# Head norms of mixers AB and C: the reciprocal root as exp of minus half the logarithm, on ScalarE

## What is computed

```python
def _head_rmsnorm(o, gain):
    o = o * lax.rsqrt(jnp.mean(o * o, axis=-1, keepdims=True) + NORM_EPS)
    return o.reshape(o.shape[0], o.shape[1], -1) * gain.astype(jnp.float32)

# mixer AB: ob = _head_rmsnorm(ob, norm_gain); y = concat([oa, ob]) * silu(gate); y @ w_out
# mixer C:  y = _head_rmsnorm(o, norm_gain) * silu(gate);                        y @ w_out
```

## Time and profile before

| | us |
|---|---|
| runs of the kernel | 2100.96, 2101.53, 2105.75; median 2101.53 |
| the profiled execution | 2103.88, of which the span from first to last instruction 2101.8 |
| mixer AB from the first scan's decays to the layer norm | about 1700 to 1804 of the span |
| mixer C | about 1804 to the end |
| mean granted PE clock over the span | 0.961 |

### The profile page before, as it was taken

One profiled execution on the slowest core, in us unless ns is written; L12 is line 12 of the kernel. 1 busy time (PEld: TensorE's weight loads), 2 busy tenths in 40 slices (PEclk: granted clock), 3 DMA queues, 4 the chain that ended last, 5 costly groups with the idle time before them and its releaser, 6 DMA issues.

```text
span 2101.8 us, 31282 instructions
## 1 busy us (share of the span) xinstructions
PE 1939.4 (92%) x12015; PEld 1628.8 (77%) x12015; DVE 1177.1 (56%) x1900; ACT 962.4 (46%) x1437; POOL 147.3 (7%) x172
## 2 busy tenths in 40 slices
PE   5999998999997999999898999899989998789996
PEld 3875665688886888888765789799878787789994
DVE  3335566343345555523545556677644578669895
ACT  3336444322224434411446555466435454566761
POOL 3010000000000222210000000022200000000000
PEclk7999999999997999999999999899999999899998
DMA  9225568233331332333340057445564333334432
GB/s 299 93 83 165 176 205 251 70 90 103 94 116 45 100 100 95 99 108 98 100 121 1 11 143 187 155 160 180 189 216 141 101 121 120 121 121 141 141 121 80
DMA packets 262663, 265.88 MB, mean 127 GB/s; under 512 B 6278, under 2 KB 230896, under 8 KB 262560
## 3 DMA queue, kind: packets, MB, share of 16 engines
q1 hardware_dynamic: 257280, 248.27, 37.9%
q0 software_dynamic: 4832, 15.06, 2.2%
q10 hardware_dynamic: 448, 1.12, 0.2%
HBM read 263.33 MB, written 1.10 MB: 126 GB/s over the span
## 4 chain that ended last, share of the span: by engine, by line
PE 74%; DVE 11%; ACT 8%; issue 3%; DMA 2%; SPq 0%; ACTq 0%; DVEq 0%; POOL 0%
PE bank L474 19%; PE bank L475 19%; PE bank L476 19%; PE bank L694 4%; PE bank L710 3%; DVE weights_fine L1743 3%; ACT weights_coarse L1100 2%; PE bank L468 2%; PE bank L521 2%; PE bank L532 2%; DMA region<-in_w_mod 2%; PE bank L701 1%; PE bank L738 1%; DVE region L2332 1%; ACT L1496 1%
## 5 line engine op out<-in xcount | busy, mean ns | idle before, releaser
L1743 DVE TENSOR_TENSOR weights_fine<-region,weights_coarse 128x2048 fp32r<-128x2048 f32 (+3 forms) x187 | 431.8, 2309 | 392.4 <-ACT weights_coarse L1100 391.7
L1100 ACT CAST weights_coarse<-region 128x2048 fp32r<-128x2048 f32 (+3 forms) x187 | 358.7, 1918 | 361.0 <-PE bank L476 340.3
L474 PE MATMUL bank<-normed_coarse,weights_coarse 128*128 128x512 f32 (+1 forms) x1088 | 368.5, 339 | 14.3 <-DVE normed_fine L1851 9.1
L475 PE MATMUL bank<-normed_fine,weights_coarse 128*128 128x512 f32 (+1 forms) x1088 | 367.4, 338 | 0.0
L476 PE MATMUL bank<-normed_coarse,weights_fine 128*128 128x512 f32 (+1 forms) x1088 | 367.3, 338 | 0.0
L474 PEld LDWEIGHTS bank<-normed_coarse,weights_coarse 128*128 128x128 f32 x1088 | 208.0, 191 | 38.2 <-issue 13.5
L475 PEld LDWEIGHTS bank<-normed_fine,weights_coarse 128*128 128x128 f32 x1088 | 208.0, 191 | 21.5
L476 PEld LDWEIGHTS bank<-normed_coarse,weights_fine 128*128 128x128 f32 x1088 | 207.9, 191 | 21.4
L474 PE MATMUL bank<-x_turned_coarse,weights_coarse 128*128 128x256 f32 x616 | 181.9, 295 | 22.5 <-DVE weights_fine L1743 17.6
L475 PE MATMUL bank<-x_turned_fine,weights_coarse 128*128 128x256 f32 x616 | 178.9, 290 | 0.0
L476 PE MATMUL bank<-x_turned_coarse,weights_fine 128*128 128x256 f32 x616 | 178.7, 290 | 0.0
(11 more groups left out here) (278 smaller groups left out, 3718.2 us busy)
## 6 DMA issues: line engine op xcount, KB each, us to landing
region<-in_w_mod SPq DMA_DIRECT2D x48, 1024.0 KB, 5.3
region<-in_w_up SPq DMA_DIRECT2D x44, 1024.0 KB, 5.1
region<-in_w_in_c SPq DMA_DIRECT2D x30, 1024.0 KB, 5.2
region<-in_w_in_ab SPq DMA_DIRECT2D x20, 1024.0 KB, 5.3
region<-in_w_in SPq DMA_DIRECT2D x32, 512.0 KB, 4.8
region<-in_w_down SPq DMA_DIRECT2D x16, 1024.0 KB, 5.1
region<-in_w_in SPq DMA_DIRECT2D x14, 1024.0 KB, 5.1
region<-in_w_in SPq DMA_DIRECT2D x16, 384.0 KB, 3.5
```

Of the source, the lines that this page charges most:

```text
L474: nc.tensor.matmul(o, sc, mc, start=first, stop=False)
L475: nc.tensor.matmul(o, sc, mf, start=False, stop=False)
L1100: nc.scalar.copy(w_co[:, p, 0:size], raw_w[:, s, 0:size]).then_inc(coarse_ready, 1)
L1743: nc.vector.tensor_tensor(w_fi[:, p, 0:size], raw_w[:, s, 0:size], w_co[:, p, 0:size].bitcast(F32), ALU.subtract).then_inc(fine_ready, 1)
```

## The change

The square root becomes a logarithm (with the same scale and bias), followed by an exponential with scale -0.5, which gives the reciprocal root at once. ACT waits for the logarithm to be written (`settle`) ahead of the exponential. The bank that holds the sums is now released by the exponential. The reciprocal on DVE is gone, the wait for the root stays where it was.

```diff
             def scan_root(V):
                 b, ps = take()
-                read(nc.scalar.activation(rsd, ps[:, :], ACT.Sqrt, scale=1.0 / V, bias=eps[:, 3:4]), b)
+                step(nc.scalar.activation(rsd, ps[:, :], ACT.Ln, scale=1.0 / V, bias=eps[:, 3:4]))
+                settle()
+                read(nc.scalar.activation(rsd, rsd, ACT.Exp, scale=-0.5), b)
                 seen[y_ready].next()
...
             def norm_roots(root):
 
                 dve.wait_ge(bank_read[root[0]], root[1])
-                link(nc.vector.reciprocal(rsd, rsd))
```

## The result

The changed kernel takes 2109.56 us (median of 9 runs, 2105.92 to 2113.5), the kernel before 2100.96 us in the same comparison (9 runs, 2098.34 to 2105.75). The ratio is 1.0041, with a 95% interval of 1.0030 to 1.0052: 0.4% slower. The profiled execution took 2111.67 us, with a span of 2109.9. The forecast was 2110, with a range of 2101 to 2116.

The account below looks back on a forecast made before the run. PE was taken as the bound in mixer C, in a loop through ACT's root and cast and DVE's fine half. Terms gave +3.2 us without the clock, +5.6 with it: +8.8, 2112.7 profiled, less 2.35, so 2110; range 2101 to 2116.

Parts of the forecast that it names:

- What bounds: In mixer C, PE waits on ACT's cast behind the root, then DVE's fine weight half; the reciprocal is off this loop.
- Prices on ACT: At each root, logarithm, table load and exponential: 2.53 us to ACT's next instruction (was 0.59), 2.73 to the norm (was 4.18).
- Mixer C, +7.0: Passes g = 0 to 3: each stall grows 1.94 us, the masking wait returns 0.19; four times, +7.0 us.
- Mixer AB, -2.9: Two roots: fine half behind the second starts 1.11 us earlier, and no clock fall at the first saves 1.79; -2.9 us.
- The clock, +5.6: PE's clock falls behind three or four of mixer C's 3.2 us stalls, 1.6 us each; +5.6 us, bounds 0 and 7.2.
- g = 4, -0.9: Mixer C's pass g = 4: DVE gains, and PE's waits of 0.7 us for masking and 0.2 for a fine half go.

Follow-up runs that it names:

- Adding to ACT alone: All eight roots by logarithm and exponential with scale +0.5, DVE's reciprocal kept; ratio 1.0084 to the kernel before.
- taking from DVE alone: The kernel before without its eight DVE reciprocals, the norms multiplying by the square root; ratio 0.9962 to the kernel before.
- mixer C alone: The new root in mixer C's six roots only, the old form kept in mixer AB; 2116.57 against 2103.44 us for the kernel before, ratio 1.0063.
- kernel with filled stalls: The changed kernel with 20 matmuls that nothing reads in each of mixer C's four stalls; ratio 1.0029 to the kernel before.
- kernel with mixer AB alone: The new root in mixer AB's two roots only, the old form kept in mixer C; 2101.03 against 2103.44 us for the kernel before, ratio 0.9986.

## Why the prediction was right

- **What bounds.** The loop PE, ACT's run of work, cast, fine half, PE was read rightly from one bracket: DVE idle for 1.21 us behind ACT's cast. Adding to ACT alone and taking from DVE alone confirm both halves of it.
- **Prices on ACT.** Forecast 2.53 us from root to cast and 2.73 to the norm; measured 2.53 and 2.73. The load was priced from two other places of the trace. The Trainium skill's rule (ScalarE: Activation LUTs, "Table sets: the hidden batching unit") that ln and exp share one load does not hold here: all eight exponentials behind a logarithm have one. Nor is the drain of 1.38 us that the Trainium skill adds to a load (ScalarE: Activation LUTs, "What ACT_TABLE_LOAD costs") there: it is 0.02 us from the end of the load at 1884.16 to the exponential.
- **Mixer C, +7.0.** The stalls came out at 3.2 us. Mis-sized was what DVE gives back: 0.43 us for each of the four waits for the masking, not 0.19, as the passes of 39.98 and, without any reciprocal, 38.04 us show. The 0.19 was the idle time alone; the wait also took away the 0.25 us by which the next matmul otherwise starts ahead of the profiled end of the one before. With 4 x 1.94 for the stalls and 4 x 0.43 back, the term is +6.0.
- **Mixer AB, -2.9.** Measured -2.7, with the fall gone.
- **The clock, +5.6.** Three of four stalls were followed by a fall, within the forecast. The profile has 3.9 us for the two falls within the three passes (1.25 and 2.62), where 1.6 each was forecast: a fall of the usual length costs 1.3 to 1.5 (in mixer C alone, passes of 41.47), but some last twice as long. The third cost 1.5 in the next stretch, by the kernel with filled stalls. Together that is 5.4.
- **g = 4, -0.9.** Without the fall the stretch behind the fourth stall gained 1.2 us, of which 0.4 are the fourth wait for the masking, counted above; so the term is -0.7. One effect was missed: the bank of the sums is released by the exponential, and PE waited 0.6 us for it. Its timeline in the changed kernel:

```profile
2051.50 0.68 PE L910 MATMUL bank<-region 128*128 128x128 f32 x4 [0.58 <-ACT region L1548]
```

- **Not foreseen:** mixer C's first stretch grew by 1.5 us, not 1.94. The kernel with mixer AB alone isolates it: 0.44 us came off this stretch with no change in mixer C. There PE's stall of 6.64 us (at 1844.40 before) was 5.17 with the new roots in mixer AB, and the clock was low over other stretches. That these move the end of the stretch is argued from the profile. An earlier entry into mixer C is not what shortens that stall: with the reciprocal kept, mixer C was entered 6.5 us later than before, and the stall was 5.18.
- **Where luck helped.** The mechanism was right, but 2110 against a median of 2109.56 is closer than the working deserves. Mixer C's term was 1.0 us too high, and the +0.6 us at the start, which has nothing to do with the roots, covers part of that. How many falls there are, and how long, was a range and not a sum. Single runs of the changed kernel lie 7.6 us apart.

## What to carry to other kernels

Work that leaves a half-idle engine is worth what the stall behind it is worth, and work that joins another half-idle engine costs what is queued behind it there: with 25 us off DVE and 21 us onto ACT, mixer AB, where both queues are on the chain, gained 2.7 us, and mixer C, where only ACT's is, lost 10.2. Before moving work between engines, look at what follows the instruction in its queue, and put whatever the bounding engine waits for ahead of it; here that move, made in mixer C, turned 0.4% slower into 0.4% faster, and with the same move at mixer AB's second root into 0.8% faster. Price a function by whether its table is already loaded at that place in the trace, not by its own duration. And price a wait by where the next instruction starts with and without it: the idle time in a profile can be less than half of what the wait costs, as with the masking.

## What the runs showed of the hardware

- A stall of 1.9 us was followed by a granted clock of 0.50 two times in four, at the same place of the program in each pass. A stall of 3.2 us was followed by it in 3 of 4, 4 of 4 and, with the reciprocal kept, 3 of 4 cases. Stalls of 0.8 us, with matmuls that nothing reads in front of them, never were (4 cases). The stall of 1.94 us at 1831.74 came back as one of 1.95 at 1829.35 in the changed kernel, and there the clock was 0.50 from 1831 to 1833 us. So the length of a stall didn't decide on a fall between 1.8 and 3.2 us.
- The runs of the changed kernel differ by 7.6 us, and the time goes with the mean clock of each run: 2113.5 us at 0.964, 2105.92 at 0.969.
- Two activations in a row with a wait between them, the second reading the first's output, start 0.03 us after each other's end when no table load lies between.
